# Attention's products a slot later and the last output tile in token halves, in a two-block fp32 network on one core

## What is computed

```python
def swa_sink_mixer(h, cos, sin, w_in, sinks, w_out):      # 4 KV heads, 4 query heads each, width 64
    q, k, v, gate = jnp.split(h @ w_in, [...], axis=-1)
    q, k = apply_partial_rope(q, cos, sin), apply_partial_rope(k, cos, sin)
    s = jnp.einsum('bnikgd,bnjkd->bnkgij', qb, kb) * (D ** -0.5)   # blocks of 128, window 128
    s = jnp.where(valid, s, -jnp.inf)
    m = jnp.maximum(jnp.max(s, axis=-1, keepdims=True), sink)
    p = jnp.exp(s - m)
    denom = jnp.sum(p, axis=-1, keepdims=True) + jnp.exp(sink - m)
    o = jnp.einsum('bnkgij,bnjkd->bnikgd', p / denom, vb)
    return (o * jax.nn.silu(gate)) @ w_out

h = h + swiglu_ffn(rmsnorm_2(h, norm_ffn_g[1]), ffn_w1[1], ffn_w3[1], ffn_w2[1])
return rmsnorm_2(h, final_g)                               # out: (512, 1024)
```

## Time and profile before

| | |
|---|---|
| time, median of 3 runs | 1945.95 us (1945.12 to 1946.46) |
| profiled execution | 1954.18 us, of it the span of the profile 1952.4 us |
| granted TensorE clock, mean over the span | 0.978 |
| busy: TensorE, VectorE, GpSimd, ScalarE | 96%, 55%, 45%, 30% |
| weight loads of TensorE | 76% |
| share of the chain that ended last: TensorE, VectorE, ScalarE | 86%, 8%, 3% |
| GpSimd's two passes over a half, mean of one | 1.16 and 1.18 us |
| attention with its output projection | some 502 to 731 us |
| last feed-forward's end, last product's start | 1938.55 us |

### The profile page before, as it was taken

How to read it: one execution, slowest core, us unless ns; L and a number is a source line. 1 busy time by engine, 2 the same in 40 slices (tenths; PEclk the granted TensorE clock), 3 DMA queues, 4 the chain that set the end, 5 groups by cost and what they waited for, 6 DMA issues and landing times.

```text
span 1952.4 us, 24790 instructions
## 1 busy us (share of the span) xinstructions
PE 1867.6 (96%) x9586; PEld 1487.7 (76%) x9586; DVE 1066.6 (55%) x1645; ACT 591.7 (30%) x1039; POOL 887.1 (45%) x896
## 2 busy tenths in 40 slices
PE   7999999898999898999999999999998899999997
PEld 5788887787777676658888888887776688888886
DVE  6888888865766646445333321347777743343212
ACT  4444445513333423042111100136656421111002
POOL 4444444353533244425555555654432355555552
PEclk9999999899999899999999999999999999999999
DMA  8767767567644456948888888886653588888874
GB/s 212 154 147 155 150 152 150 121 161 157 129 104 104 93 135 148 225 99 182 196 190 197 191 182 198 199 188 137 130 130 75 121 183 190 198 190 197 181 187 108
DMA packets 212836, 309.90 MB, mean 159 GB/s; under 512 B 22480, under 2 KB 166768, under 8 KB 212720
## 3 DMA queue, kind: packets, MB, share of 16 engines
q0 software_dynamic: 42624, 148.65, 44.6%
q1 hardware_dynamic: 165680, 154.28, 25.4%
q10 hardware_dynamic: 4416, 5.39, 1.1%
HBM read 153.12 MB, written 2.10 MB: 79 GB/s over the span
## 4 chain that ended last, share of the span: by engine, by line
PE 86%; DVE 8%; ACT 3%; issue 2%; ACTq 0%; DMA 0%; DVEq 0%
PE gp L699 22%; PE gp L701 22%; PE gp L700 22%; PE gp L671 2%; PE gp L673 2%; PE gp L672 2%; PE mp L949 1%; PE gp L644 1%; PE gp L645 1%; PE gp L646 1%; PE mp L1025 1%; DVE m_xs L1756 1%; PE mp L886 1%; PE mp L910 1%; PE mp L821 1%
## 5 line engine op out<-in xcount | busy, mean ns | idle before, releaser
L593 POOL TENSOR_SCALAR wh<-stage 128x1024 fp32r<-128x1024 f32 (+2 forms) x298 | 346.7, 1163 | 940.5 <-PE gp L701 737.1
L699 PE MATMUL gp<-hh,wh 128*128 128x512 f32 x1512 | 606.8, 401 | 5.1 <-DVE m_raw L1706 4.3
L700 PE MATMUL gp<-hh,wl 128*128 128x512 f32 x1512 | 591.5, 391 | 0.0
L701 PE MATMUL gp<-hl,wh 128*128 128x512 f32 x1480 | 579.9, 392 | 0.0
L599 POOL TENSOR_SCALAR wl<-stage 128x1024 fp32r<-128x1024 f32 (+2 forms) x296 | 350.2, 1183 | 0.0
L699 PEld LDWEIGHTS gp<-hh,wh 128*128 128x128 f32 x1512 | 285.8, 189 | 73.1 <-issue 15.0
L700 PEld LDWEIGHTS gp<-hh,wl 128*128 128x128 f32 x1512 | 286.2, 189 | 58.6 <-issue 1.4
L701 PEld LDWEIGHTS gp<-hl,wh 128*128 128x128 f32 x1480 | 279.5, 189 | 60.1
L602 POOL DMA_DIRECT2D wl<-stage x296 | 262.7, 888 | 94.1 <-POOL wl L599 83.4
L2139 DVE TENSOR_TENSOR val<-gp,rstd 128x512 f32<-128x512 f32 x44 | 30.4, 692 | 203.8 <-PE gp L701 203.8
L699 PE MATMUL gp<-f_h,wh 128*128 128x512 f32 x352 | 137.2, 390 | 0.0
(11 more groups left out here) (358 smaller groups left out, 2742.0 us busy)
## 6 DMA issues: line engine op xcount, KB each, us to landing
wl<-stage POOLq DMA_DIRECT2D x263, 512.0 KB, 5.4
stage<-ffn_w SPq DMA_DIRECT2D x120, 512.0 KB, 4.2
stage<-ssm_w_in SPq DMA_DIRECT2D x32, 512.0 KB, 5.0
stage<-hg_w_in SPq DMA_DIRECT2D x32, 512.0 KB, 4.5
stage<-ssm_w_in SPq DMA_DIRECT2D x32, 256.0 KB, 5.0
stage<-ssm_w_out SPq DMA_DIRECT2D x16, 512.0 KB, 3.8
stage<-att_w_in SPq DMA_DIRECT2D x16, 512.0 KB, 4.4
stage<-cp_w_in SPq DMA_DIRECT2D x12, 512.0 KB, 5.3
```

The lines of the kernel that those rows point to most:

```text
L593: pool.tensor_scalar(wh[:, s, part], stage[:, s, part], 1.0, 1.0, ALU.mult, ALU.mult).then_inc(hi_done, 1)
L699: pe.matmul(bank[:, :], wvh[:, cols], hi(kk), start=start, stop=False)
L700: pe.matmul(bank[:, :], wvl[:, cols], hi(kk), start=False, stop=False)
L701: mm = pe.matmul(bank[:, :], wvh[:, cols], lo(kk), start=False, stop=stop)
```

## The change

**Attention.** The granules yield at a quarter tile (k = 2, 4, 6), 6 products each. A round has twelve slots on TensorE: quarters 2 in slots 0 to 8, then 1, 0, 1 in rounds 1 and 2; 2, 2, 1, 1, 2, 1, 1, 2, 2, 1, 0, 1 in round 3; in round 4 four quarters in slots 0 to 2 and twelve granules of the output projection in slots 3 to 11. `turn_p(i)` goes to slot i + 3 and ahead of that slot's scores, `pv(i)` to slot i + 4. ScalarE's `copy_p(i)` moves to slot i + 3, the highs to 9 and 12, the gates to 8 and 12 (the last gate tile: slot 7 of round 4). VectorE's `gate_o(0)` moves from slot 6, ahead of the mask, to slot 8, behind `normalise` and a `take`; the rotations move to slots 2, 4, 8 (2, 5, 8 in round 3), the takes to 1, 3, 5, 7, 11 (1, 4, 7, 11 in round 3).
**The end.** The last column group of the last feed-forward is cut into two of 128 columns, each with units of 16 and 6 row blocks. Tile 7 is made by `last_tile` in two halves of 256 tokens in two banks; in the first lies `turn_out(6)`, in the second the transposes and the sums of the first half; the same for the second half follow. The squares of tile 7 go into the sums directly. Ln and Exp become Sqrt, its table loaded ahead, and a reciprocal on VectorE, for each half; scaling and output follow each half.

```diff
-        for n in range(D // UC):
+        for n in range(D // UC - i):
             add(f"down{i}", w["w2"][i], [(0, n * UC, UC)], [(0, 8), (8, 8), (16, 6)])
+        for n in range(6, 6 + 2 * i):
+            add(f"down{i}", w["w2"][i], [(0, n * P, P)], [(0, 16), (16, 6)])
...
-    direct = (1, 2, 3, 4)
+    direct = (1, 2, 3, 4, 8)
...
-                            if k == un.kt // 2:
+                            if k and k % (un.kt // parts) == 0:
                                 yield
-                                if m == 0:
-                                    weights_whole(u, 1)
+                            if m == 0 and k == un.kt // 2:
+                                weights_whole(u, 1)
...
+                fills = [(2, 2, 1, 1, 1, 1, 1, 1, 1, 1, 1, 1)] + 2 * [(2, 2, 2, 2, 2, 2, 2, 2, 2, 1, 0, 1)]
+                fills += [(2, 2, 1, 1, 2, 1, 1, 2, 2, 1, 0, 1), (1, 2, 1, 2, 1, 1, 1, 1, 1, 1, 2, 2)]
                 for h in range(KVH + 1):
...
+                    for k in range(12):
+                        run(gran_out if h == KVH and k > 2 else gran, fills[h][k])
                         if h:
+                            if 0 <= k - 3 < 8:
+                                turn_p(h - 1, k - 3)
                             if k < 8 and k % 2 == 0:
                                 scores(h - 1, k // 2)
-                            if 0 <= k - 2 < 8:
-                                turn_p(h - 1, k - 2)
-                            if 0 <= k - 3 < 8:
-                                pv(h - 1, k - 3)
+                            if 0 <= k - 4 < 8:
+                                pv(h - 1, k - 4)
...
+            def last_tile():
+
+                u0, t = phases["down1"][1] - 2, out_tile("down1", KT - 1)
+                for half in range(2):
+                    tokens = slice(half * UC, (half + 1) * UC)
+                    bank = gp[(t + half) % 4]
+                    pe.wait_ge(bank_read[(t + half) % 4], (t + half) // 4)
+                    for u in (u0, u0 + 1):
+                        un = units[u]
+                        for k in range(un.kt):
+                            if half == 0 and k in (0, un.kt // 2):
+                                weights_whole(u, int(k > 0))
+                            if u == u0 and k == KT:
+                                if half == 0:
+                                    turn_out(KT - 2)
+                                else:
+                                    turn_half(0)
+                                    sum_half(0)
+                            wvh, wvl = weights_at(u, k)
+                            high, low = gh[:, un.k0 + k, tokens], gl[:, un.k0 + k, tokens]
+                            pe.matmul(bank[:, 0:UC], wvh[:, :], high, start=u == u0 and k == 0, stop=False)
+                            pe.matmul(bank[:, 0:UC], wvl[:, :], high, start=False, stop=False)
+                            mm = pe.matmul(bank[:, 0:UC], wvh[:, :], low, start=False,
+                                           stop=u > u0 and k == un.kt - 1)
+                    mm.then_inc(last_half, 1)
+                turn_half(1)
+                sum_half(1)
...
+                    act.activation(root[:, rows], mp[3 - half][:, 0:2], ACT.Sqrt, bias=eps_col[:, 0:1],
+                                   scale=1.0 / D).then_inc(root_ready, 1)
...
+                take_at = KVH * [(1, 3, 5, 7, 11)]
+                rope_at = KVH * [(2, 4, 8)]
+                take_at[KVH - 1], rope_at[KVH - 1] = (1, 4, 7, 11), (2, 5, 8)
                 for h in range(KVH + 1):
...
+                        if h and k == 8:
+                            gate_o(h - 1, 0)
```

More of the change, by code:

```diff
@@ L1117, in _ @@
             hgrn()
-            ffn(1, 5, turn_out)
-            pe.wait_ge(sq_added, adds_before(pre_round[6] + 1))
-            for c in range(NCH):
-                mm = pe.matmul(mp[3][:, c:c + 1], sqsum[:, c * P:(c + 1) * P], ones[:, 0:1], start=True, stop=True)
-            mm.then_inc(sum_ready, 1)
+            ffn(1, 5)
+            last_tile()
         @block.scalar
@@ L1543, in last_norm @@
                 r = pre_round[6]
-                for k in range(KT):
+                for k in range(KT - 1):
                     x_wait(act, 6, k)
@@ new lines, in attention @@
+                    for k in range(13):
+                        if h and k < 8:
+                            if k % 2:
+                                normalise(h - 1, k // 2)
+                            else:
+                                mask_scores(h - 1, k // 2)
+                        if h and k == 8:
+                            gate_o(h - 1, 0)
+                        if h < KVH:
+                            if k in take_at[h]:
+                                take(h, take_at[h].index(k))
+                            if k in rope_at[h]:
+                                rope(h, rope_at[h].index(k))
+                        elif k == 3:
+                            take(h - 1, 4)
+                        if h and k == 11:
+                            gate_o(h - 1, 1)
+                        if h < KVH and k == 12:
+                            copy_v(h)
+                        if h and k in (9, 12):
+                            n = 2 * (h - 1) + (k == 12)
+                            low(split0["att"] + n, oh[:, n, :], ol[:, n, :])
@@ L2026, in add_to_x @@
             def add_to_x(name, v):
-                for k in range(KT + 1):
-                    if k < KT:
+                for k in range(KT + (v != 6)):
+                    if v == 6 and k == KT - 1:
+                        add_square(dve, pre_round[v], k - 1)
+                    elif k < KT:
                         t = out_tile(name, k)
@@ L2330, in _ @@
             ffn(1, 5)
-            dve.wait_ge(rstd_ready, pre_round[6] + 1)
-            for c in (0, 2):
+            for half in range(2):
+                t, col = out_tile("down1", KT - 1), P_FINAL + KT - 1
+                tokens, rows = slice(half * UC, (half + 1) * UC), slice(2 * half, 2 * half + 2)
+                dve.wait_ge(last_half, half + 1)
+                dve.tensor_tensor(xT[:, KT - 1, tokens], gp[(t + half) % 4][:, 0:UC], xT[:, KT - 1, tokens],
+                                  ALU.add).then_inc(last_x, 1)
+                dve.wait_ge(last_x, half + 1)
+                dve.wait_ge(out_turned, KT - 2)
+                dve.tensor_scalar(val[:, 1, tokens], xT[:, KT - 1, tokens], prm[:, col:col + 1], None,
+                                  ALU.mult).then_inc(value_ready, 1)
+                dve.wait_ge(root_ready, half + 1)
+                dve.reciprocal(rstd[:, rows], root[:, rows]).then_inc(rstd_ready, 1)
+                dve.wait_ge(rstd_ready, pre_round[6] + 1 + half)
+                c = 2 * half
                 dve.tensor_scalar(rows_out[:, c, :], rows_out[:, c, :], rstd[:, c:c + 1], None,
```

114 lines of the change are left out of this document (54 added, 60 removed).

## The result

Timed in the same rounds, the changed kernel took 1932.28 us in the median of four runs (1929.79 to 1935.42), the kernel before 1945.53 (1944.39 to 1946.46): 13.25 us less, a ratio of 0.9926 with a 95% interval of 0.9913 to 0.9938. Forecast were 1927.0 us and a range of 1920.5 to 1936.5. The time lies in the range and the sign was right; the gain is two thirds of the 19.2 us forecast.

What follows compares the result with a forecast made beforehand. TensorE was taken as the bound, with time to win in attention's waits and slow clock and in the tail. Attention -17.2 and last tile -2.0 made -19.2 us off the median of 1945.95: 1927 us, range 1920.5 to 1936.5.

Steps and rivals of the forecast that it cites:

- What bounds the kernel: Whole kernel: TensorE bounds it; gains lie in attention's waits (some 20.5 us), clock (10 us) and the 13.4 us tail.
- The end of the kernel: Last tile in two token halves: +0.9 + 2.1 + 0.3 - 5.3 = -2.0 us, ends -3.5 and +7.2.
- (b): Last tile: weight loads set the pace of the halves, 24.9 us instead of 15.8, 1936 us; chance 0.07.
- (c): Last tile: 256-token products fall to the f32 rate, 0.43 us each, 41 us more, 1968 us; chance 0.04.
- The tail: From the last add to the end of the kernel: 8.1 us instead of 13.4, -5.3.
- what comes ahead of the last add: Last tile: +0.9 us for half products, +2.1 for turns and sums, +0.3 for a weight wait.
- The later slot and the quarters: Attention: heads gain 6.6, 5.0, 1.6 and 5.0 us, together 18.2, taken as 17.2; ends 10 and 21.
- The walk: Attention: the three engines' queues followed slot by slot with uncontended times, giving 18.2 us gained, margins 0.25 to 1 us.
- the term of 1 us for contention: Attention: 1 us off the 18.2 us gain because VectorE operations stretch when GpSimd works beside them.
- Rival (a): Attention: VectorE's stretches and ScalarE's copies behind exponentials keep a third of the waits, gain 10 us, 1934 us; chance 0.17.
- Rival (d): Attention: VectorE's chain sets the head's period; new waits at value product 4 and turn 1, 1944 us; chance 0.05.
- From profile to median: Whole kernel: profiled execution 8.2 us above the median 1945.95; the same 19.2 us taken off the median, giving 1927.

Runs made afterwards that it cites:

- end_only: Only the last-tile part of the change, with its norm and weight pieces, in the kernel before: 1946.84 us, ratio 0.9989.
- after_again: The changed kernel, unchanged, timed and profiled a second time against the kernel before: 1934.55 us, ratio 0.9929.
- before_again: The kernel before, unchanged, timed against itself and profiled a second time: 1946.6 us, ratio 1.0001.
- gate_early: Changed kernel with VectorE's `gate_o` moved from slot 8 to slot 7, ahead of the normalise: 1926.74 us, ratio 0.9888 to the kernel before.
- exps_late: Changed kernel with ScalarE's exponentials one slot later, behind that slot's copy: 1933.79 us, ratio 0.9922 to the kernel before.
- slot_only: Changed kernel with attention's weight products in halves again, turns and value products still one slot later: 1943.29 us, ratio 0.9981 to the kernel before.
- att_only: Only the attention part of the change in the kernel before, last tile as before: 1939.28 us, ratio 0.9947.
- att_again: Only the attention part of the change in the kernel before, repeated on another chip: 1935.86 us, ratio 0.9937.
- both_take: Changed kernel with earlier `gate_o`, later exponentials and the last round's last gate take ahead of the second normalise: 1914.04 us, ratio 0.9832 to the kernel before.

## Why the prediction was right, and where it fell short

*What bounds the kernel.* Right. The 15.5 us on the normalise went, and removing waits of TensorE in attention goes on paying down to 3.7 us of them.

*The end of the kernel.* Held. Forecast -2.0; measured -2.1 by the ratio (0.9989, with an interval from -4.7 to +0.4), -3.3 in the traces. Products of 256 tokens at 0.12 us apart: exact, so rivals (b) and (c), at 0.189 and 0.43 us, are out. From the end of the turns at 1905.39 to the last start 17.3 us, where 132 x 0.12 and the turns and sums in between make 17.8 by the prediction's terms. The tail was 7.75 us (`end_only` 7.76) for 8.1 forecast, 5.7 less than before. The step that was a little too dear is what comes ahead of the last add: forecast +3.3, and from HGRN's first output product to the last add `after_again` is 2.4 us longer than `before_again` (425.2 and 422.8), `end_only` 2.4 longer than the first profile of before (430.6 and 428.1; that pair has the HGRN wait in both). TensorE had no wait on weights there.

*The later slot and the quarters.* The kinds of waits and their producers were forecast, and in heads 3 and 4 most of the turns that they hit; the sizes were not. A wait of over 2 us at a turn of P, which the prediction said would not come, came in head 3 (2.2). By head, forecast gain and then the gains of the two pairs of profiles: head 1 6.6, and 5.5 and 5.1; head 2 5.0, and 3.7 and 3.7; head 3 1.6, and -4.5 and -1.2; head 4, net of the 0.7 us of work moved behind it, 5.0, and 4.0 and 2.6 (its period shrank by 4.7 and 3.3, and what follows grew by 0.7). Three errors make it up.

1. *Turn 3 in heads 1 and 2.* The walk took turn 1 for the closest, with 0.25 us to spare, and wrote "all else is early". Turn 1 was early; turn 3 waited 1.4 us in both heads. In the changed kernel's head 1 VectorE did this ahead of the mask of slot 4 (the mask starts at 537.81):

```profile
529.65 0.76 DVE L2020 STREAM_SHUFFLE a_rtmp<-a_qraw 128x512 f32<-128x512 f32 x1
530.29 0.80 DVE L2021 TENSOR_TENSOR a_rtmp<-a_qraw,a_cos 128x512 f32<-128x512 f32 x1
531.02 1.52 DVE L2023 TENSOR_TENSOR a_rtmp<-a_rtmp,a_sin 128x512 f32<-128x512 f32 x1
532.58 3.25 DVE L2025 TENSOR_TENSOR a_qr<-a_rtmp 128x512 f32<-128x512 f32 x1
532.91 1.37 POOL L596 TENSOR_SCALAR wh<-stage 128x1024 fp32r<-128x1024 f32 x1
533.92 1.37 POOL L602 TENSOR_SCALAR wl<-stage 128x1024 fp32r<-128x1024 f32 x1
535.76 0.15 DVE L1984 TENSOR_TENSOR a_srow<-a_srow 128x4 f32<-128x4 f32 x1
```

   The rotation took 6.1 us (529.65 to 535.76) where the walk had 2.55, by the same stretching of VectorE that the earlier trace rows showed: GpSimd made two pairs of passes from 529.51 to 535.29, and none beside the rotation of the earlier trace rows. This was no chance of one execution. In all nine profiles that have these slots and counts (those of the changed attention, and those with `gate_early`'s or `exps_late`'s edit or more) the first rotation took 6.1 us in the rounds of heads 1 and 2 and 4.7 in that of head 3; in both profiles of before, where it stands in slot 4, it took 2.6, 2.6 and 3.3. So it belongs to the new order. That GpSimd causes it rests on the overlap in time alone; `slot_only`, with the rotations in the same slots and other counts, had 6.1, 4.1 and 2.6, and no run moved a rotation by itself. The scores were there at 534.15 (532.67 + 1.48), and the mask of a block that the walk starts 0.2 us behind them started 3.7 behind. The step that failed is the term of 1 us for contention: one such stretch is 3.5 us, it comes in three heads, and it was taken off the sum instead of being put into the queue, where it could be seen that it meets a copy standing behind exponentials. The walk priced the moved rotation by a row from another place, where nothing ran beside it.
2. *Head 3.* Forecast 3.7 us of waits, measured 6.0 and 5.4 (5.4 and 7.5 in `att_only` and `att_again`), of which turn 3 alone 2.15 in the second profile instead of 0.75. The forecast also held that no piece would be long enough to draw the clock down and left 0.6 us for it. In the first profile it granted 0.89, in the second 0.96. So the head that was to gain 1.6 lost 1.2 to 4.5.
3. *The clock.* Granted clock of 0.97 or more was forecast for all four windows. It holds for heads 1 and 2 (1.00), and fails for head 3. In head 4 it was 1.00 in the first profile and 0.96 in `after_again`, `att_only` and `att_again`.

The waits were 14.3 to 16.2 us over the four profiles of the changed attention, against 9.9 forecast, some 5 us more; the stretch gained about 9 instead of 17.2. So some 5 of the 8 us missing are waits. The rest would be the clock behind them; that division is read off, not tested.

*Rival (a)*, "the margins are eaten", at 1934 with 0.17, is the case that came: its text names ScalarE's copies behind exponentials, its 10 us for attention is what the two runs gave (10.3 and 12.3), and its time is 2 us from the median. The time lies in the stated range because the range took in this rival, and the extra 1.3 us of the end helped. The argument against it, that heads 1 and 2 lose their hole outright, was true of the hole and overlooked what would be late next. *Rival (d)* put the whole head under VectorE's chain: no, since `both_take` reaches 43.1 us with the same VectorE work. It was the order of the queues that counted, not the amount of work in them.

*From profile to median.* The sum was taken off the median unchanged. That was right: the long execution of the first profile cost 5.5 us in HGRN, outside the windows on which the sum rests, and attention agreed to 0.7 us in the second profile. The sentence that "nothing says that its waits are longer than a plain run's" was wrong all the same for the HGRN wait, and would have done harm if that wait had been counted as removable.

## What to carry to other kernels

When a chain through two helper engines is moved later, write down for every queue what stands in front of each item that the bound engine will need, and ask for each whether it waits on somebody else: an item that is ready must not stand behind one that still waits (the copy behind the exponentials, `gate_o` and the bank's reader behind the normalise). Such edits cost nothing and brought 13.5 us of the attention stretch here (19 by the ratios, part of it in stages that scatter), more than the change itself, but they had to be made together: by itself the later start of the exponentials gave nothing, since it moved the wait to the next producer. And spread the filler so that no slot is empty before moving anything later, since the later slot gave nothing with the halves tried here. Where an operation is moved, look at what will run beside it in its new place: the rotation's time was read where GpSimd was idle, and with GpSimd's passes beside it in its new place it took more than twice as long.

## What the runs showed of the hardware

Two things were not expected. In HGRN a VectorE operation of 0.69 us took 3.18 us and the next 2.59 instead of 0.78 in three of the fourteen profiles and in no other; in attention a rotation of 2.55 us took 6.1 in heads 1 and 2 of all nine profiles with the change's slots and counts. GpSimd's passes over weights ran beside both. In HGRN they did so in the short case too: in the two profiles of before, one starts 0.24 us after the first operation each time (at 1542.72 and at 1542.45). Why the one execution stretches the operation is left open. Its cost is not small: from HGRN's first output product to the end, 5.2 of the 5.5 us between the two profiles of before. Whether it also explains that plain runs of that kernel lie between 1944.6 and 1953.9 us is not shown.

The second is how much the clock adds to a wait. The same order of work gave a head of 44.97 us at a granted 0.96 and one of 48.21 at 0.89, with only 0.6 us more of waits. A third profile of the same order had 47.20 us at 0.96, with 7.5 us of waits. A forecast for such a stretch should carry these values as its range, not one.
